# Slabs of the stages without attention in twos: high products of two slabs, then their low products

## What is computed

```python
D_MODEL, SEQ, DEPTH, D_FF, FFN_K, PLE_DIM = 2048, 256, 2, 5632, 3, 256
# first block, layer i
x = x + jnp.concatenate([y_a, y_b, y_c, y_d], axis=-1) @ w_o[i]
uf = causal_dwconv(rmsnorm(x, g_ffn[i]) @ w_up[i], w_ffn_conv[i])
gate, up = jnp.split(uf, 2, axis=-1)
x = x + (jax.nn.silu(gate) * up) @ w_down[i]
pe_gate = jax.nn.sigmoid(rmsnorm(x, g_pe[i]) @ w_pg[i])
x = x + (p[i] @ w_pe[i]) * pe_gate
...
# second block, layer l
x = x + jnp.einsum("bse,ed->bsd", mixed, w_out)
```

## Time and profile before

| | before |
|---|---|
| median of 3 runs | 3351.33 us (3349.7 to 3352.63) |
| the profiled execution, time of the run | 3352.41 us |
| its span in the profile | 3350.2 us |
| PE busy | 3327.6 us, 99% |
| DVE busy | 2617.8 us, 78% |
| ACT busy | 1531.6 us, 46% |
| granted TensorE clock, mean | 0.998 |
| high products, line 642, on H and on G | 6496 and 1408 matmuls |
| low products, line 653, on H and on G | 6624 and 1408 matmuls |

### The profile page before, as it was taken

One profiled execution on the slowest core, in us unless ns is written; L12 is line 12 of the kernel. 1 busy time (PEld: TensorE's weight loads), 2 busy tenths in 40 slices (PEclk: granted clock), 3 DMA queues, 4 the chain that ended last, 5 costly groups with the idle time before them and its releaser, 6 DMA issues. The chain is left out here.

```text
span 3350.2 us, 53769 instructions
## 1 busy us (share of the span) xinstructions
PE 3327.6 (99%) x20366; PEld 2929.1 (87%) x20366; DVE 2617.8 (78%) x3394; ACT 1531.6 (46%) x1642; POOL 864.2 (26%) x633
## 2 busy tenths in 40 slices
PE   9999999999999999999999999999999999999998
PEld 8989888888888989888888888888888888888897
DVE  8897788787786888887887787867867866678865
ACT  5644444343433556544443434335444444445443
POOL 0422432121122423414332121214432004150004
PEclk9999999999999999999999999999999999999999
DMA  6445555555555554455555555555544455544454
GB/s 241 148 163 176 189 188 189 178 202 177 206 174 189 203 182 165 151 176 187 190 188 178 198 180 199 180 190 200 193 164 153 167 173 189 180 164 151 167 185 151
DMA packets 90647, 605.21 MB, mean 181 GB/s; under 512 B 10192, under 2 KB 10352, under 8 KB 29296
## 3 DMA queue, kind: packets, MB, share of 16 engines
q1 hardware_dynamic: 89424, 599.83, 52.0%
q10 hardware_dynamic: 1056, 3.11, 0.2%
HBM read 600.80 MB, written 2.10 MB: 180 GB/s over the span
## 5 line engine op out<-in xcount | busy, mean ns | idle before, releaser
L642 PE MATMUL bank<-H,whi 128*128 128x512 f32 x6496 | 1574.3, 393 | 1.5 <-DVE z L1661 1.5
L1164 ACT ACTIVATE whi<-raw 128x2048 fp32r<-128x2048 f32 (+2 forms) x609 | 1093.6, 1796 | 1044.6 <-DMA raw<-in_slabs_down 259.8
L1630 DVE TENSOR_TENSOR wlo<-raw,whi 128x2048 fp32r<-128x2048 f32 (+2 forms) x609 | 1328.4, 2181 | 243.2 <-ACT whi L1164 233.1
L642 PEld LDWEIGHTS bank<-H,whi 128*128 128x128 f32 x6496 | 1188.7, 188 | 238.6 <-issue 5.9
L653 PEld LDWEIGHTS bank<-H,wlo 128*128 128x128 f32 x6624 | 849.1, 188 | 34.3
L653 PE MATMUL bank<-H,wlo 128*128 128x256 f32 x6624 | 871.1, 281 | 0.0
L511 POOL TENSOR_TENSOR sqtmp<-tmp 128x256 f32<-128x256 f32 x88 | 218.9, 2488 | 867.8 <-DVE tmp L2211 867.8
L642 PE MATMUL bank<-G,whi 128*128 128x512 f32 x1408 | 343.0, 391 | 0.0
L642 PEld LDWEIGHTS bank<-G,whi 128*128 128x128 f32 x1408 | 255.4, 188 | 48.0
L1564 ACT ACTIVATE G<-sqtmp 128x256 f32 (+1 forms) x88 | 36.8, 418 | 404.0 <-POOL sqtmp L511 404.0
L489 POOL TENSOR_TENSOR sqacc<-sqacc,sqtmp 128x256 f32<-128x256 f32 x119 | 199.4, 1676 | 9.4
(11 more groups left out here) (390 smaller groups left out, 2881.4 us busy)
## 6 DMA issues: line engine op xcount, KB each, us to landing
raw<-in_slabs_up SPq DMA_DIRECT2D x176, 1024.0 KB, 4.8
raw<-in_slabs_down SPq DMA_DIRECT2D x128, 704.0 KB, 4.0
raw<-in_slabs_wo SPq DMA_DIRECT2D x32, 1024.0 KB, 4.8
raw<-in_slabs_pg SPq DMA_DIRECT2D x32, 1024.0 KB, 4.9
raw<-in_slabs_gates SPq DMA_DIRECT2D x32, 1024.0 KB, 4.9
raw<-in_slabs_wout SPq DMA_DIRECT2D x32, 1024.0 KB, 4.8
raw<-in_slabs_sc SPq DMA_DIRECT2D x24, 1024.0 KB, 4.8
raw<-in_slabs_fox SPq DMA_DIRECT2D x24, 1024.0 KB, 4.9
```

The lines of the kernel that those rows point to most:

```text
L642: pe.matmul(b[0:r.m, :], whi[:, n % RAW, w], r.src[:, k, :], start=at == 0, stop=False)
L1164: act.activation(whi[:, n % RAW, 0:w], raw[:, n % RAW, 0:w], ACT.Copy).then_inc(S("hi_ready"), 1)
L1630: dve.tensor_tensor(wlo[:, n % RAW, 0:w], raw[:, n % RAW, 0:w], whi[:, n % RAW, 0:w].bitcast(F32), ALU.subtract).then_inc(S("lo_ready"), 1)
```

## The change

PE's program alone changes. In a stage with a loop, every slab but the first two of a `high_first` stage and the last two of the stage goes through two new functions: `high_row` issues the waits and the high products of one slab, `low_row` those of the low ones. The high products are issued slab by slab; the low products of both slabs of a pair (j = 0, 1 and j = 2, 3) stand behind the high products of the second. The number of instructions and of waits is the same. The call that runs the work beside `pg` (`advance`) moves along: it stands at three quarters of a low row and at its end.

```diff
+        def high_row(r, i, j, operand, order, free):
+            n = r.first + j
+            pe.wait_ge(S("hi_ready"), n + 4 * i + 1)
+            pe.wait_ge(S("evac"), bank_free.get(n + 4 * i, n + 4 * i - 3) if isinstance(i, int) else n + 4 * i - 3)
+            if free is not None:
+                free(j)
+            for at in range(r.kt):
+                k = at if order is None else order[at]
+                if operand is not None and j == 0 and (i == 0 if isinstance(i, int) else r.loop):
+                    operand(k)
+                pe.matmul(bank_of(r, n)[:], whi[:, n % RAW, k * P:k * P + P], r.src[:, k, :], start=at == 0, stop=False)
+
+        def low_row(r, i, j, order, beside):
+            n = r.first + j
+            pe.wait_ge(S("lo_ready"), n + 4 * i + 1)
+            for at in range(r.kt):
+                k = at if order is None else order[at]
+                if at == r.kt * 6 // 8:
+                    advance(beside, 1)
+                last = pe.matmul(bank_of(r, n)[:, 0:T], wlo[:, n % RAW, k * P:k * P + P], r.src[:, k, 0:T],
+                                 start=False, stop=at == r.kt - 1)
+            last.then_inc(S("slab_done"), 1)
+            advance(beside, 1)
...
                 if high is not None and isinstance(i, int) and 4 * i + j < 2:
                     continue
+                if r.loop and not (isinstance(i, int) and 4 * i + j >= r.count - 2):
+                    high_row(r, i, j, operand, order, free)
+                    if j % 2:
+                        low_row(r, i, j - 1, order, beside)
+                        low_row(r, i, j, order, beside)
+                    continue
```

## The result

The kernel after takes 3361.46 us (median of 15 runs, 3356.29 to 3366.31), the kernel before beside it 3352.63 (3349.70 to 3353.93). The ratio is 1.0024, with a 95% interval of 1.0017 to 1.0031: slower by 0.24%, small but clear of no change. I had forecast 3347.0, a gain of 4.3 us. The profiled execution of after took 3362.01, its span is 3359.8, the mean granted clock 0.998 as before.

A forecast was written before the change was run, and what follows sets the result against it. PE, busy 99%, was taken to bound the kernel by its matmul rate. 172 pairs at 0.025 us gain 4.3, new waits cost nothing: 3351.33 - 4.3 = 3347.0 us; 8-in-10 range 3344.0 to 3353.5.

The forecast's parts named there:

- the rate: On PE, each pair drops one step from low to high products, gaining 0.025 us (ends 0.01 and 0.035).
- Rival 1: No gain: a high row's start may cost the same whatever precedes it on PE; 3351.3 us, chance 0.10.
- 172 pairs: Count of pairs over wo, up, down, pg and wout; at 0.025 us each, a gain of 4.3 us.
- The spares for up and down: Time left before PE needs its inputs in these loops: 3.1 to 5.65 us in up, 1.9 to 4.4 in down.
- The norm's sum in pg: At pg's start it moves by 3.65 us; the low split behind it was still covered by 0.9.
- the last two slabs of each stage stay as they are, so the next stage's inputs are no later: At stage ends, unpaired last slabs keep the next inputs on time; new PE waits cost nothing.
- 10.2 of 11.08 us a pair: DVE's need per pair in up against the pair's length, so its backlog does not grow.
- at worst 2.5 later: In down, two loads issued 1.30 us apart may share DMA engines; the odd one keeps 1.9 us spare.
- Rival 2 in its milder form: PE stands at some ten stage changes, 1.5 us each; names into up 2, up 0; about 3362, slower by more 0.07.
- 1.9 or more everywhere: Argument against slower outcomes: the estimate keeps this spare in us everywhere with worst load sharing, but for pg.
- its own 1.85: Spare in us at the change into up 2: 4.37 less 2.52.
- The prediction is wrong if a wait of PE on hi_ready or lo_ready adds up to more than 2 us: Refutation sign in the profile after: PE's waits on these two signals should stay at nothing in the loops.

The follow-up runs named there:

- e13: The change kept only in up 0 to 3, down 0 to 2 and, below slab 12, wo and wout (146 pairs): 3347.58 us, ratio 0.9984 to before.
- e1: The change kept only in up 0 to 3 and down 0 to 2 (126 pairs): 3348.46 us, ratio 0.9991 to before.
- e7: The change with wo, wout and down 3 paired only below slab 12, pg only in slabs 0 to 3 (162 pairs): 3352.53 us, ratio 0.9998 to before.
- e11: The kernel before, no pairs, with loads of wo, down 3, wout and the first slab behind them issued in twos: 3363.28 us, ratio 1.0036.
- e14: The kernel before, no pairs, with six needless DVE products behind slab 12 of pg, about 3.0 us in all: 3356.19 us, ratio 1.0015.

## Why the prediction was wrong

**Right: the rate.** Steps from low to high products cost what the starts showed. 0.025 us a pair was forecast, 0.0275 measured (after: 4.9 us in the loops for 178 pairs; e13: 4.2 for 146). It splits otherwise than I had it: 0.033 for a pair of 16 chunks (11.080 to 11.047) and 0.020 for one of down (7.627 to 7.607), where I had priced down's the higher. Rival 1, no gain, is refuted. The rule of the Trainium skill ("TensorE: Matmul & The Clock Gate", section "Back-to-back issue gap") that the prediction names is the page's formula for an isolated matmul; by it the order would be worth nothing, and it does not hold for these rows. The second high row of a pair takes 3.626 us, 0.2266 a matmul from its start.

**Slightly wrong: the count.** I took 172 pairs; there are 178. In down 0 to 2 the loop's `i` is a register up to the last slab, so the exception for the last two slabs never applies. That is worth 0.1 us and no loss: e1 has those pairs.

**Right: the loops.** The spares for up and down held with loads in twos: no wait of PE on `hi_ready` or `lo_ready` in any loop, neither in after nor in e1. The norm's sum in pg was covered too.

**Wrong: "the last two slabs of each stage stay as they are, so the next stage's inputs are no later. New waits of PE I therefore cost at nothing".** This step failed, twice over. That PE's own last two rows stay doesn't keep the engines behind it on time:

- I worked out DVE's need in up, 10.2 of 11.08 us a pair, and never in pg. There it is 5.35 of 5.54, and DVE starts 5.6 us late, which a row of pg's start would have shown, had I read it (its reciprocal at 1126.51 stands between the norm's sum and the low split of the earlier trace rows). With 0.2 us to make up per slab, much of an early pair's 3 to 4 us lives on to the last slabs (1.9 in e7), and the last pair's 2.8 does so whole. Price: 2.7 + 3.2 us.
- For the loads I allowed "at worst 2.5 later" inside down, and never asked what loads are on the way when down 3 or wo ends: those of the next stage. There the second of the two came 3.6 us (8.5 - 4.9) later after its issue, in a place whose spare I had not read and where it was 0.3 to 0.4. Price: 3.4 + 2.2 us behind down 3, 0.8 + 1.8 + 0.5 behind wo and wout.

Together 14.5 us, which the sum held at 0. Rival 2 in its milder form named the kind (stands at the changes of stage, +15 - 4.3, 3362) and nearly the time. That the time came out so near is luck: it had ten places with 1.5 us each, the traces have seven with 0.5 to 3.4, and at one of the two that it names, into up 2, nothing was lost. Its chance of 0.07 came from an estimate that had "1.9 or more everywhere", with the loops and two changes of stage read and the others not; even its own 1.85 is below that. "The prediction is wrong if a wait of PE on hi_ready or lo_ready adds up to more than 2 us" also looked at the wrong signals: PE's new waits in the list are 2.3 + 1.0 + 0.7 us, for a copy, a bank and `H`, and 0.8 without a releaser, and behind pg the loss is hardly a wait at all but matmuls that stand 0.40 us apart in place of 0.24.

## What to carry to other kernels

Before engines are made to hand over in pairs, work out for each stage how much of a slab's time its second-busiest engine needs and how late it starts: where that leaves 0.2 us in 5.5, what a batch delays is largely still there at the stage's end and is paid one for one, and a page that says 78% busy doesn't show it. A change that only moves work inside a loop must be costed at the loop's exits: what is loading, and whose input is still being made. And a mechanism is confirmed quickest by making it in the kernel before, without the change (e11, e14); where a delay varies by itself, compare its size with the loss at each place, as with the loads here.

## What the runs showed of the hardware

- Two loads of 1 MB close together: in after the first of two takes 4.9 us from issue to landing in the median, as one alone does, and the second, issued 1.3 to 1.9 us behind it, 5.4 to 8.4, median 6.6 (122 loads). In e11, 0.4 to 0.6 behind, it takes 6.6 to 8.5. Of 704 KB one alone takes 4.0, the second of two (52 loads, 1.3 behind) 5.3 to 6.5, median 5.7. I had expected both to lose a little; the first loses nothing.
- The slowness outlasts the pair: behind the loads of pe in after the next two of each layer, each 3.8 us behind the one before, take 6.7 to 7.1 us, where before's 1 MB loads at that spacing took 4.6 to 5.3.
- A high row of 16 matmuls of 512 columns takes 3.626 us when it follows another one and 3.652 when it follows a low row (after, up 1).
- DVE's product of 128x256 behind the evacuation in pg takes 0.42 us when POOL stands still and 0.93 when POOL's sum of the same size begins just ahead of it. Of the 32 such products of e14, the 26 that run beside a POOL instruction take 0.93 or 0.94 and the other six 0.42. It is a pattern of the traces, not tested by itself. Both in the timeline of e14, the first behind the six needless products:

```profile
1198.51 0.42 DVE L2226 TENSOR_TENSOR tmp<-tmp,rms 128x256 f32<-128x256 f32 x1
...
1203.05 0.74 POOL L489 TENSOR_TENSOR sqacc<-sqacc,sqtmp 128x256 f32<-128x256 f32 x1
...
1203.13 0.93 DVE L2226 TENSOR_TENSOR tmp<-tmp,rms 128x256 f32<-128x256 f32 x1
```
